# Patterns for the gates: one VectorE comparison of 512 columns for four tokens, in place of 256 columns on VectorE and two comparisons on GpSimd

## The reference, cut to what matters

```python
def peer(h, w_q, sub_keys, u_tab, v_tab):
    experts, gates = peer_route(hf, w_q, sub_keys)      # expert = i1 * 128 + i2
    a = jnp.einsum('td,tkd->tk', hb, u_tab[eb])
    w = gb.astype(hb.dtype) * jax.nn.gelu(a, approximate=False)
    return jnp.einsum('tk,tkd->td', w, v_tab[eb])
```

## Time and profile before

| | |
|---|---|
| median of 3 runs | 4752.36 us |
| the profiled execution's own time | 4750.15 us |
| its span (first to last instruction) | 4748.3 us |
| PE / DVE / ACT / POOL busy | 86% / 77% / 37% / 24% |
| DVE line 2172 (second patterns) | 768 instructions, 229.6 us |
| DVE line 2169 (first patterns, tokens 0 and 1) | 192 instructions, 79.2 us |
| POOL line 1163 (first patterns, tokens 2 and 3) | 384 instructions, 251.2 us |
| POOL lines 1158 and 1161 (keys copied) | 192 instructions |

### The profile page before, as it was taken

The page is one execution under the profiler, slowest core; times in us unless marked ns, Lnnn a source line. Parts: engine busy times, 40 slices in busy tenths (PEclk is TensorE's granted clock), DMA queues, the critical chain, the costliest instruction groups (busy, mean ns, idle before and its releaser), DMA issues. The chain is left out here.

```text
span 4748.3 us, 68020 instructions
## 1 busy us (share of the span) xinstructions
PE 4088.8 (86%) x22885; PEld 3537.4 (74%) x22885; DVE 3641.2 (77%) x7170; ACT 1752.8 (37%) x3127; POOL 1135.6 (24%) x1190
## 2 busy tenths in 40 slices
PE   6967876799879999999999967688682799999998
PEld 5966434699768888888888857533462799999998
DVE  3158566489989999999999932834499899999998
ACT  3222642210334444444444332254321444444443
POOL 0000000000774343344443300000003723333332
PEclk8965988895899999999999988599896999999999
DMA  4110112114569999999999911000121799999997
GB/s 163 54 36 27 36 54 88 32 50 133 160 218 373 371 375 376 374 380 374 380 376 369 374 54 32 1 17 0 58 67 43 239 371 372 372 374 374 374 372 283
DMA packets 246331, 1018.03 MB, mean 214 GB/s; under 512 B 16976, under 2 KB 115376, under 8 KB 145984
## 3 DMA queue, kind: packets, MB, share of 16 engines
q0 software_dynamic: 85824, 602.70, 32.8%
q1 hardware_dynamic: 160320, 413.17, 24.5%
HBM read 963.31 MB, written 52.43 MB: 214 GB/s over the span
## 5 line engine op out<-in xcount | busy, mean ns | idle before, releaser
L475 PE MATMUL psA<-h_hi,split_hi 128*128 128x448 f32 (+3 forms) x2816 | 984.9, 350 | 163.0 <-DVE h_lo L1684 64.6
L1187 POOL DMA_INDIRECT rows<-rows,pick_i x512 | 794.6, 1552 | 1155.1 <-DVE y_tok L2219 644.1
L1666 DVE TENSOR_TENSOR split_lo<-raw,split_hi 128x1024 fp32r<-128x1024 f32 x596 | 727.9, 1221 | 388.9 <-ACT split_hi L1228 386.8
L475 PE MATMUL psA<-h_lo,split_hi 128*128 128x448 f32 (+3 forms) x2816 | 965.1, 343 | 0.0
L475 PE MATMUL psA<-h_hi,split_lo 128*128 128x448 f32 (+3 forms) x2816 | 965.1, 343 | 0.0
L1228 ACT ACTIVATE split_hi<-raw 128x1024 fp32r<-128x1024 f32 x596 | 628.2, 1054 | 403.1 <-PE psV L475 172.5
L475 PEld LDWEIGHTS psA<-h_hi,split_hi 128*128 128x128 f32 x2816 | 533.5, 189 | 240.8 <-issue 121.4
L2207 DVE CUSTOM_DVE_ANT_1 rows<-rows,h_wide 128x1024 f32<-128x1024 f32 x512 | 624.5, 1220 | 9.2 <-DMA rows<-rows,pick_i 6.8
L2219 DVE SCALAR_TENSOR_TENSOR y_tok<-rows,pick_w,y_tok 128x1024 f32<-128x1024 f32 x444 | 569.0, 1281 | 5.9
L475 PEld LDWEIGHTS psA<-h_lo,split_hi 128*128 128x128 f32 x2816 | 534.3, 190 | 35.7
L475 PEld LDWEIGHTS psA<-h_hi,split_lo 128*128 128x128 f32 x2816 | 533.0, 189 | 37.2
(11 more groups left out here) (301 smaller groups left out, 6704.5 us busy)
## 6 DMA issues: line engine op xcount, KB each, us to landing
raw<-expert_pairs SPq DMA_DIRECT2D x256, 1024.0 KB, 7.2
gates<-g_buf SPq DMA_DIRECT2D x24, 2048.0 KB, 8.7
raw<-tiles SPq DMA_DIRECT2D x84, 512.0 KB, 3.5
raw<-mod_tiles SPq DMA_DIRECT2D x80, 512.0 KB, 3.5
g_in<-gates POOLq DMA_DIRECT2D x32, 896.0 KB, 9.0
g_in<-gates POOLq DMA_DIRECT2D x32, 640.0 KB, 5.8
mod_w<-mod_pairs SPq DMA_DIRECT2D x8, 1024.0 KB, 17.8
rows<-rows,pick_i POOLq DMA_INDIRECT x512, 8.5
```

Of the source, the lines that this page charges most:

```text
L475: ins = nc.tensor.matmul(out_, lhsT, rhs, start=start, stop=stop)
L1187: nc.gpsimd.indirect_dma_start(rows[l][:, b, :], None, (rows0, rows1)[l], bass.IndirectOffsetOnAxis(pick_i[:, u:u + 1], 0))\
L1666: V.tensor_tensor(split_lo[:, n % SPLIT].rearrange("p k n -> p (k n)"), raw[:, n % RAW, :], split_hi[:, n % SPLIT].rearrange("p k n -> p ( ...
```

## The change

The 512 columns of four first patterns come from one DVE comparison. GpSimd makes none: its loop, its buffer `first_key`, its chain semaphore and the semaphore `oh_first` go, and PE no longer waits for the latter. The buffer `first_key` was 32 bytes per partition, so what is placed behind it in SBUF lies 32 bytes lower.

```diff
@@ PE, build_gates
-                seen.enter(i, {oh_ready: 2 * GROUPS, oh_first: 2 * GROUPS, psum_A_free: 2 * GROUPS})
+                seen.enter(i, {oh_ready: 2 * GROUPS, psum_A_free: 2 * GROUPS})
                 for g in range(2 * GROUPS):
-                    pe.wait_ge(oh_first, seen.upto(oh_first))
                     pe.wait_ge(oh_ready, seen.upto(oh_ready))
@@ POOL
             tb0, tb1 = gate_blocks(l)
-            pool.wait_ge(sel_copied, seen.upto(sel_copied, NTT - DENSE[l][0] // P))
...
-            nc.gpsimd.tensor_copy(first_key[:, 0], idxT[:, 0, tb0 * TB + 2:tb0 * TB + 4]).then_inc(pool_chain, 1)
-
-            def first_one_hots(i, last):
...
-                    for j in range(2):
-                        ins = nc.gpsimd.tensor_scalar(onehot[:, g % 4, 0, 2 + j], iota, first_key[:, g % 4, j:j + 1], None,
-                                                      ALU.is_equal)
-                    ins.then_inc(oh_first, 1)
...
             for b in range(2):
                 pool.wait_ge(g_stored[b], seen.upto(g_stored[b], 16 * (tb1 - tb0) // 2))
@@ DVE, build_gates
                     t = i * (2 * TB) + (tb0 * TB + 4 * g)
-                    V.tensor_tensor(onehot[:, g % 4, 0, 0:2], iota.unsqueeze(1).broadcast_to([P, 2, P]),
-                                    idxT[:, 0, bass.ds(t, 2)].unsqueeze(2).broadcast_to([P, 2, P]), ALU.is_equal)
+                    V.tensor_tensor(onehot[:, g % 4, 0, 0:4], iota.unsqueeze(1).broadcast_to([P, 4, P]),
+                                    idxT[:, 0, bass.ds(t, 4)].unsqueeze(2).broadcast_to([P, 4, P]), ALU.is_equal)
                     for j in range(4):
```

More of the change, by code:

```diff
@@ L178, in build_program @@
     act_chain = semaphore("act_chain")
-    pool_chain = semaphore("pool_chain")
     dve_chain = semaphore("dve_chain")
@@ L247, in build_program @@
     oh_ready = semaphore("oh_ready")
-    oh_first = semaphore("oh_first")
     oh_passed = semaphore("oh_passed")
@@ L281, in build_program @@
     small = place("small", [P, 160])
-    first_key = place("first_key", [P, 4, 2])
     ident2 = place("ident2", [P, HALF])
@@ L1144, in _ @@
             tb0, tb1 = gate_blocks(l)
-            pool.wait_ge(sel_copied, seen.upto(sel_copied, NTT - DENSE[l][0] // P))
-            base = 3 + l * (DENSE[0][1] // TB) * GROUPS
-            steps = (tb1 - tb0) // 2 - 1
-            nc.gpsimd.tensor_copy(first_key[:, 0], idxT[:, 0, tb0 * TB + 2:tb0 * TB + 4]).then_inc(pool_chain, 1)
-            def first_one_hots(i, last):
[L1152 to L1161, removed]
-                    for j in range(2):
-                        ins = nc.gpsimd.tensor_scalar(onehot[:, g % 4, 0, 2 + j], iota, first_key[:, g % 4, j:j + 1], None,
-                                                      ALU.is_equal)
-                    ins.then_inc(oh_first, 1)
[L1167 to L1171, removed]
             for b in range(2):
```

## The result

The kernel after takes 4782.85 us, the median of 4 runs (4781.86 to 4783.41). The kernel before, with a fourth run, takes 4753.48 us (4748.3 to 4758.6). The ratio is 1.0062, with a 95% interval of 1.0044 to 1.0079, so the change costs 29 us, 0.6% (21 to 38 us by the interval). The profiled execution took 4782.45 us, its span is 4780.5 us.

A forecast was written before the change was run, and what follows sets the result against it. DVE was taken to bound the gate stages; its period of 1.36 + 0.267 = 1.627 us added 17.9 and 15.7 us, together 33.6, to 4750.15, giving 4783.8, as a median 4785 us. The 8-in-10 range was 4776 to 4803.

The forecast's parts named there:

- The step from 4783.8 by 2.2 us to a median: Whole kernel: the profiled execution stood 2.2 us below the median of runs, so 4783.8 became a median of 4785 us.
- The sum of 33.6 us: Both gate stages: 17.9 us slower in layer 0 plus 15.7 in layer 1, all on the path.
- DVE sets the pace: Gate stages: DVE is full and the next group waits for it; PE and ACT have room, POOL runs beside.
- The removal gives back 0.11 and 0.07 us a group: Gate stages, layers 0 and 1: without POOL's instructions DVE's group falls from 1.467 and 1.431 to 1.36 us.
- Two places in the earlier trace: Layer 0: four patterns spanning 1.10 us in the last group; a 0.26 us step before 1227.25, where POOL sat idle.
- 256 columns cost 0.267 us: DVE's comparison, 192 times: 256 more columns add 0.267 us, priced from longer fp32 two-tensor operations.
- Period and sum: Gate stages: new period 1.36 + 0.267 = 1.627 us; layer 0 grows 17.9 us, layer 1 15.7, together 33.6.
- Nothing else moves: Outside DVE's groups: last store's 8.94 us wait stays, buffer shift counts zero; 5 us either way allowed for it and clock.
- The rival that the disturbance stays: Gate stages: the 0.11 and 0.07 us are DVE's own and not given back; 51.3 us slower, 4803; chance 0.05.
- The rival of PE at the lower clock: Gate stages: clock falls for most of them, PE sets a 1.7 us period; 47.6 us slower, 4800 to 4802; chance 0.05.
- The rival of much shorter patterns: DVE's second patterns: without POOL a step falls to 0.125 us, PE becomes the bound; -58 us, 4694; chance 0.04.
- The rival that nothing is seen: Behind the stage: something already late, a weight load or store, swallows the delay; time stays at 4752; chance 0.04.

The follow-up runs named there:

- the first experiments: Four kernels: the removal alone; the addition alone; one POOL pattern a group with 384 DVE columns, 4771.1 us; the addition alone with POOL memsets, 4788.59 us (four further runs).
- the removal alone: Kernel after, with DVE comparing only 256 columns and nobody making first patterns of tokens 2 and 3 (zeroed once a layer): 4735.56 us, ratio 0.9959 to the kernel before.
- the addition alone: Kernel before, with DVE comparing 512 columns while POOL still makes its two patterns, into a buffer nobody reads: 4804.33 us, ratio 1.0103.

## Why the prediction was right

It was right: 4785 us against 4782.85, its range held, and slower had the chance of 0.92. The nearness of the single number is better than its working. The step from 4783.8 by 2.2 us to a median gives 4786, not 4785, and the median of the kernel before moved by 1.1 us with its fourth run. The sum of 33.6 us is to be compared with 33.4 us of the stages in the profiles, and with 29 us of the medians. By its steps:

- *DVE sets the pace.* Shown: DVE is full in both stages after, and PE's waits are for DVE alone. The period moved by what the steps of DVE's instructions moved, within 0.01 us, in the change and in the first experiments. Where DVE's patterns went to others, POOL became the bound in two kernels, in one no engine was full, and in one DVE stayed the bound.
- *The removal gives back 0.11 and 0.07 us a group.* Shown. An undisturbed group of 256 columns was forecast at 1.36 us, and is 1.36 with the removal alone. Over 192 groups this is 17.7 us; the stages became 17.3 us shorter with the removal alone, and the time 20 (the interval is 13 to 26, and the zeroing is in it). Two places in the earlier trace rows were enough to tell it. The second is weaker than the prediction says: POOL is at work for the first 0.48 us of the four patterns that span 1.10. It still told the right number, as no instruction of POOL starts in it, and it is behind such a start that the other rows have their longer steps.
- *256 columns cost 0.267 us.* Shown: 0.602 - 0.335 = 0.267 in the change, 0.268 and 0.265 in the addition alone. (The rows that it was taken from give 958 - 692 = 266 ns.)
- *Period and sum.* Forecast 1.627 us in both layers, measured 1.628. The stages were forecast to grow by 17.9 and 15.7 us, and from first to last comparison they grew by 17.8 and 15.5.
- *Nothing else moves.* The store's wait at the end is 8.96 us against 8.94. Outside the stages the two profiles differ by 1 us, within the 5 us allowed; but this is the balance of pieces of 1.5 to 2.8 us, and the move of the buffers by 32 bytes and the clock in the later stages were not tried by themselves. By medians the change cost 29.4 us, against 33.6 of the sum; the interval of the ratio (21 to 38 us) holds both, and two runs of one kernel differ by several microseconds.
- *The rival that the disturbance stays* falls with the removal alone. The addition alone shows what it would have given: 4804, the rival's 4803.
- *The rival of PE at the lower clock* falls with the granted clock of 1.00 at 71% busy in the profile after.
- *The rival of much shorter patterns* falls with a step of 0.256 us without any POOL. The Trainium skill, page "SBUF — State Buffer", section "SBUF: two separate sides", describes an exclusive lock on the ports that VectorE and GpSimd share, under which the one that starts first has them for its whole instruction and the other is blocked; a VectorE instruction with two SBUF inputs, as the comparison is, meets it only beside a GpSimd instruction that reads SBUF, a condition that the prediction left out. The traces agree with it on POOL's side: with one pattern a group POOL's instruction stretches from 0.594 to 1.175 us, by about the 0.55 of the comparison inside it, and memsets, which read nothing, leave the period at 1.63. They do not agree on DVE's side: it loses 0.055 us per POOL instruction, and no group of the kernel before is longer than 1.49 us, where one lost POOL instruction of 0.6 would make it 1.96. Read by that rule alone the change would have been a large gain; the rows decide, and they had said so beforehand.
- *The rival that nothing is seen* falls with the time.

What stays open: why the two engines are aligned in layer 0 so that both of POOL's starts cost DVE 0.055 us and in layer 1 so that one does (it is so in the addition alone too, by its periods), and what in POOL's instruction causes the loss.

## What to carry to other kernels

When a full engine hands work to one beside it, or takes it back, price the work on the full engine by the columns it costs there, and price the helper's side effect apart: here 0.267 us against 0.11. The side effect can be read without an experiment, at the places where the helper happens to stand still while the full engine runs on. And a helper's busy share is no measure of what it can take: ACT was busy 0.4 of the stage, and every kernel that moved gates to it or to POOL was slower or no faster, by POOL's instructions stretched beside DVE or by engines waiting for each other.

## What the runs showed of the hardware

- Each value per partition costs a 128x128 fp32 instruction of DVE 0.061 us: steps of 0.135, 0.196 and 0.256 us with none, one and two. On POOL the second one, with its multiplication, costs 187 ns at the least (minimum of 781 against 594).
- Beside a full DVE, a POOL comparison of 128 columns takes between 0.59 and 1.6 us, by what of DVE it meets: the median is 0.663 in the kernel before, 0.708 beside comparisons of 512 columns and 1.175 with one pattern a group, where it starts just ahead of the comparison. DVE loses 0.055 us at one step behind a POOL start, or nothing. POOL memsets of that size cost DVE nothing in the typical group.
- On ACT a multiplication of 128 columns by a value per partition takes 0.39 us, two in a row 0.69, and 0.20 us of idle time stand between an eviction and the next of them.
